# Sampled tokens' attention: all loads of cached values on SyncE's queue, between the key loads

## The reference

```python
def dilated_sample(q_a, k_a, v_a, k_buf, v_buf):      # branch A: 12 query heads, 4 K/V heads
    qg = q_a.reshape(DB, T, N_GROUPS_A, HEADS_PER_GROUP_A, HEAD_DIM)
    for g, (win, dil) in enumerate(DIL_PAIRS):         # (128, 1), (512, 4), (2048, 16)
        o, lse = dilated_gather_group(qg[:, :, g], k_a, v_a, k_buf, v_buf, win, dil)
    return merge_groups(outs, lses, q_a.dtype)

def dsa_sample(q_b, k_b, v_b, q_i, k_i, w_i, pool_k, pool_v, pool_ik, page_table):
    sc = ...                                           # indexer scores, the top 256 keys of each query
    ks = pool_k[phys, off]                             # branch B: paged cache, 8 query heads, 2 K/V heads
    vs = pool_v[phys, off]
    return sparse_attend(q_b, ks, vs, valid & (idx < P), k_b, v_b, sel_new)

o = (softmax(q k^T * HEAD_DIM ** -0.5 + mask)) @ v     # what each branch computes
x = x + gate * ((sigmoid(g_a) * ((o_a * silu(z_a)) @ w_pa) + sigmoid(g_b) * ((o_b * silu(z_b)) @ w_pb)) @ w_out)
```

## Time and profile before

| | us |
|---|---|
| median of 3 runs | 3146.28 |
| lowest and highest | 3145.56, 3151.08 |
| the execution that was profiled | 3147.91 |
| its span on the core | 3146.0 |
| PE busy in the span | 3054.7 (97%) |
| DVE, ACT, POOL busy | 1693.4, 749.9, 266.7 |
| stage of the sampled tokens | 2320 to 2461 |

### The profile page before, as it was taken

How to read it: one execution, slowest core, us unless ns; L and a number is a source line. 1 busy time by engine, 2 the same in 40 slices (tenths; PEclk the granted TensorE clock), 3 DMA queues, 4 the chain that set the end, 5 groups by cost and what they waited for, 6 DMA issues and landing times. The chain is left out here.

```text
span 3146.0 us, 50501 instructions
## 1 busy us (share of the span) xinstructions
PE 3054.7 (97%) x19803; PEld 2881.1 (92%) x19811; DVE 1693.4 (54%) x2463; ACT 749.9 (24%) x1173; POOL 266.7 (8%) x516
## 2 busy tenths in 40 slices
PE   5989999999999999999999999999999999999998
PEld 4869999999999999999999999988876897998986
DVE  4573786200786355555455554566654544654755
ACT  5240000011000111211111111165433323333333
POOL 3100000000000000000000000042224101010000
PEclk8999999999999999999999999999999999999999
DMA  9832222222222222333233232565269774683672
GB/s 350 282 114 70 75 74 61 82 61 61 82 75 61 94 63 75 105 93 102 75 95 109 81 102 75 181 198 147 85 188 312 215 269 158 194 269 127 207 237 98
DMA packets 452309, 425.08 MB, mean 135 GB/s; under 512 B 20628, under 2 KB 393620, under 8 KB 449108
## 3 DMA queue, kind: packets, MB, share of 16 engines
q1 hardware_dynamic: 428998, 343.06, 36.8%
q0 software_dynamic: 22048, 78.45, 6.7%
q10 hardware_dynamic: 1152, 2.13, 0.2%
HBM read 348.79 MB, written 76.88 MB: 135 GB/s over the span
## 5 line engine op out<-in xcount | busy, mean ns | idle before, releaser
L293 PE MATMUL banks<-h_hi,w_hi 128*128 128x352 f32 (+1 forms) x3552 | 1162.5, 327 | 0.0
L295 PE MATMUL banks<-h_hi,w_lo 128*128 128x352 f32 (+1 forms) x3552 | 1158.3, 326 | 0.0
L294 PE MATMUL banks<-h_lo,w_hi 128*128 128x352 f32 (+1 forms) x3552 | 1157.4, 326 | 0.0
L293 PEld LDWEIGHTS banks<-h_hi,w_hi 128*128 128x128 f32 x3552 | 666.8, 188 | 3.1 <-issue 3.0
L294 PEld LDWEIGHTS banks<-h_lo,w_hi 128*128 128x128 f32 x3552 | 669.2, 188 | 0.0
L295 PEld LDWEIGHTS banks<-h_hi,w_lo 128*128 128x128 f32 x3552 | 666.2, 188 | 0.0
L284 DVE TENSOR_TENSOR w_lo<-w_raw,w_hi 128x2048 fp32r<-128x2048 f32 x77 | 175.4, 2278 | 657.3 <-ACT w_hi L279 519.6
L372 ACT ACTIVATE col<-banks 128x384 f32<-128x384 f32 x150 | 71.2, 474 | 1023.6 <-PE banks L295 984.0
L1944 DVE TENSOR_TENSOR u_lo<-u_raw,u_hi 128x1536 fp32r<-128x1536 f32 (+1 forms) x96 | 196.4, 2046 | 200.4 <-ACT u_hi L1858 200.0
L2216 DVE MAX8 best<-work 128x8 f32<-128x1088 f32 x224 | 289.1, 1291 | 10.0
L2218 DVE MATCH_REPLACE8 work<-best,work 128x1088 f32<-128x1088 f32 x224 | 285.9, 1276 | 0.0
(11 more groups left out here) (313 smaller groups left out, 3432.0 us busy)
## 6 DMA issues: line engine op xcount, KB each, us to landing
w_raw<-in_w_in SPq DMA_DIRECT2D x76, 1024.0 KB, 5.5
u_raw<-in_w_out SPq DMA_DIRECT2D x96, 512.0 KB, 5.0
scratch_proj<-col POOLq DMA_DIRECT2D x76, 544.0 KB, 3.0
ada_w<-in_w_ada SPq DMA_DIRECT2D x16, 2048.0 KB, 13.9
u_raw<-in_w_pb SPq DMA_DIRECT2D x48, 512.0 KB, 4.9
gate_w<-in_w_ada SPq DMA_DIRECT2D x16, 1024.0 KB, 7.8
u_raw<-in_w_pa SPq DMA_DIRECT2D x48, 256.0 KB, 3.1
gates<-scratch_proj SPq DMA_DIRECT2D x64, 192.0 KB, 2.4
```

What stands on the lines that cost most here:

```text
L293: nc.tensor.matmul(dst, w_hi[:, par, k, 0:width], h_hi[:, k, a:b], start=(k == 0), stop=False)
L294: nc.tensor.matmul(dst, w_hi[:, par, k, 0:width], h_lo[:, k, a:b], start=False, stop=False)
L295: mm = nc.tensor.matmul(dst, w_lo[:, par, k, 0:width], h_hi[:, k, a:b], start=False, stop=(k == KT - 1))
```

## The change

Value sets 1 to 6 are issued by SP and no longer by POOL. SP's order becomes keys 2, values 1, keys 3, values 2, and so on to keys 7, values 6; o_raw, z_raw and values 7 follow as before. Values b still wait for `so_done` >= b-1, now in SP's queue; values 1 wait for `pv_done`, the end of the prompt's value products, for which POOL waited before it. All value sets count on one pair of semaphores, and PE waits on it for (half + 1) sets of the buffer, half being the sequence number divided by 2. POOL keeps `prepare`. The transfers, their sizes and destinations are the same, and PE's, ACT's and DVE's work too.

```diff
@@ load_values
             if not isinstance(b, int) or b >= 2:
                 sp.wait_ge(so_done, b - 1)
-            by_sp = isinstance(b, int) and b in (0, NB - 1)
-            load_rows(sp, b, par, (win_v, "cache_win_v"), (pool_v, "cache_v"), v_raw_landed if by_sp else v_next_landed)
+            load_rows(sp, b, par, (win_v, "cache_win_v"), (pool_v, "cache_v"), v_raw_landed)
@@ sp_sample
-            for b in range(2, NB):
+            load_keys(sp, 2, 0)
+            sp.wait_ge(pv_done, NJ)
+            load_values(sp, 1, 1)
+            for b in range(3, NB):
                 load_keys(sp, b, b % 2)
+                load_values(sp, b - 1, (b - 1) % 2)
             sp.wait_ge(att_stored[0], 16 * QT // 2)
@@ pool_sample
             prepare(1, 1, 0, False)
-            load_values(pool, 1, 1)
             with pool.Fori(1, NB // 2 - 1) as i:
                 for u in range(2):
                     prepare(2 * i + u, u, i, False)
-                    load_values(pool, 2 * i + u, u)
             prepare(NB - 2, 0, NB // 2 - 1, False)
-            load_values(pool, 2 * (NB // 2 - 1), 0)
             prepare(NB - 1, 1, NB // 2 - 1, False)
@@ pe_sample, body
-                if isinstance(b, int) and b in (0, NB - 1):
-                    pe.wait_ge(v_raw_landed[par], RAW)
-                else:
-                    pe.wait_ge(v_next_landed[par], (half + par) * RAW)
+                pe.wait_ge(v_raw_landed[par], (half + 1) * RAW)
```

More of the change, by code:

```diff
@@ L1269, in decode_step @@
         v_raw_landed = [sem(f"v_raw_landed{i}") for i in range(2)]
-        v_next_landed = [sem(f"v_next_landed{i}") for i in range(2)]
         prep_set = sem("prep_set")
```

## The result

| | us |
|---|---|
| changed kernel, median of 4 runs | 3177.23 (3173.99 to 3179.71) |
| kernel before, median of 4 runs | 3147.14 (3145.56 to 3151.08) |
| ratio | 1.0093, 95% interval 1.0080 to 1.0106 |
| changed kernel, the execution profiled, its span | 3173.99, 3172.1 |

The changed kernel is slower by 25 to 33 us (the interval of the ratio, in us). The forecast was 3173 us, +26.5, with a range of 3163 to 3186.

The account below looks back on a forecast made before the run. SP's issuing, 11.3 us a set, was taken to become the attention stage's bound. First matmul of the merge +25.5 us, from pace and tail, plus 1 for the clock: +26.5 on 3146.3, giving 3173 us, range 3163 to 3186.

Parts of the forecast that it names:

- The bound passes to SP's issuing: Sampled tokens' attention: SP needs 22.6 us per sequence against PE's 16.2, so its issuing replaces PE and DMA engines as bound.
- The new waits cost nothing: SP's queue: waits on so_done and pv_done are already met when SP reaches them, so they add no time.
- Which sets come late: Attention stage: keys 3 in time, values 2 at 2371.0 (wanted 2370.6), keys 4 at 2382.3 (wanted 2377.8), each set after waited for.
- The tail: After o_raw's issue at 2458.9: o_raw, z_raw and values 7, 7.34 MB at 362 GB/s, landing at 2480; term -6 to +10.
- pace: SP's issuing from keys 2 on: 12 sets at 11.3 us, 135.6 us, ending at 2458.9; term -2.4 to +13.
- From values 7 to the merge: From sequence 7's value products at 2480 to the merge's first matmul at 2487, +25.5 us against 2461.5 before.
- the 1 us for the clock: Allowance for slower PE work after waits, not hidden behind the last wait, before values 7: 1 us, between 0 and 4.
- Rival 1: Attention stage: DMA engines stay the bound, the queue is of no account, 3144 to 3152 us; chance 0.05.
- Rival 2: Attention stage: issuing sets in order of use saves 7 us, 3139, if SP issues a set under 8.1 us; chance 0.05.
- Rival 3: Attention stage: SP's sets stretch to 17.2 us each as in the kernel before, 71 us more, 3244 us; chance 0.07.
- The rule weighed: For these sets, issuing (11.3 us) outlasts moving (8.7 us at 302 GB/s), against the rule that sequencer time is usually small.

Follow-up runs that it names:

- What was added to the queue: Changed kernel, but SP loads each page number of value sets 1 to 6 into a register twice: 3204.81 us, ratio 1.0177 to the kernel before.
- fixed pages: Changed kernel with constant page numbers and no register loads from sequence 1 on, so other pages of the same size are read: 3155.33 us, ratio 1.0017.
- registers reused: Changed kernel, but page numbers loaded once per sequence, at its key set, serve its value set too: 3156.16 us, ratio 1.0027; again 3157.92 us, 1.0028.

## Why the prediction was right

- **The bound passes to SP's issuing: right.** Set pace 11.37 us against 11.3, 136.4 us for the 12 sets against 135.6. What was added to the queue (27 us) came through as 24 to 26 us, and of what was taken from it (o_raw 22.8 us sooner) 21 us were gained, so this is shown.
- **The new waits cost nothing: right.** SP shows no wait on `so_done` between keys 2 and o_raw.
- **Which sets come late: right for the keys, wrong for the values.** Keys 3 in time, values 2 late by 0.44 us where 0.4 was worked out, keys 4 by 5.05 where it was 4.5. But PE never waited for values 3 to 6, and I had said that it would. PE needs 9.8 us from the turning to the values' products at full clock; after each wait the 24 transposes took 4.5 to 5.4 us and not 2.8, which makes 11.6 to 12.5 us, over SP's 11.37. The slow clock took the place of the second wait. It changed nothing in the sum, since SP sets the pace.
- **The tail: mis-sized.** From o_raw's issue to the start of the values' products of sequence 7 I had 21.1 us, from 7.34 MB at 362 GB/s. It was 26.2 (2456.35 to 2482.58). In 2456 to 2483 the engines moved 8.55 MB at 317 GB/s:

```profile
DMA packets 7142, 8.55 MB, mean 317 GB/s; under 512 B 324, under 2 KB 6500, under 8 KB 7140
GB/s 138 59 194 71 337 398 400 403 416 360 364 369 373 375 369 373 376 371 373 371 378 374 353 230 241 176 224 285 331 349 355 361 349 355 339 321 297 294 292 275
```

  So two things were left out. 1.2 MB more moved, mostly the end of values 6 and the start of u_raw, which SP issued from 2476 on. And 362 GB/s held only from the fifth of these 40 slices to the 23rd, where o_raw and z_raw moved; the first four (2.7 us) stood at 59 to 194, and the five behind them, where by the order of the queue values 7 begin, at 176 to 285. This term is 5.1 us short. From the forecast's +26.5 one comes to the measured +30.5 of the stage with pace +0.8, tail +5.1, and -1.9 of the next item.
- **From values 7 to the merge: right, a little high.** 6.1 us, against 7 and the 1 us for the clock. That 1 us does not show: the first products of sequence 7 took 2.79 us, against 2.34 before, both partly or wholly at the lower level.
- **Rival 1, no difference:** what it needs is a set in 8.7 us. With fixed pages SP issued the first sets in 6.8 and 7.4 us, the DMA share was 1.04 again, and the loss 2 to 9 us. As a mechanism it is nearly right once SP keeps up, and that was not the case here. **Rival 2, use order:** its condition, SP's own pace under 8.1 us, was met in that same kernel and nothing was gained; the lower rate there leaves open what the order is worth by itself. **Rival 3** did not occur in the changed kernel, whose sets never stretched while the engines were not full. With fixed pages, where the engines were full, they did stretch, to 9.8 us each (2333.99 to 2431.99, ten sets).
- **The rule weighed** (the Trainium skill, DMA: Bandwidth & Descriptors, "Issuing engines are not separate DMA queues"): that all issuing engines feed the same 16 DMA engines agrees with a share of 1.04 from SP's queue alone, and with the 2 to 9 us that the queue still made once issuing was cheap. That the issue time is usually small was not so for these sets: 11.3 us to issue what the engines move in 8.7, eight pages of 128 KB, each behind a register load.

**Open.** Why the value sets on SP's queue cost another 2 to 9 us with the issuing out of the way. The rate goes with it: 277 GB/s with nothing on POOL, 284 with a fifth of the bytes, 292 to 295 with 45% or more. Packet size alone does not give this row (1.83 and 1.87 KB stand for 284 and 295, and 2.11 for 292), and neither does the number of queues in use, which is two in all but the first. How the two queues share the engines was not tried by itself.

## What to carry to other kernels

Before transfers are gathered on one engine, add up what it takes that engine to issue them, register loads included, and compare the sum per step with the step of the engine that waits; below it such moves cost 1 to 9 us here and not 30, above it what was added showed nearly in full. A queue's own timeline in a stretch where nothing blocks it gives this pace, and busy times do not show it at all. And a wait removed by another order of the same bytes can turn up again at the transfer that is now last, as it did twice here, with z_raw.

## What the runs showed that was not expected

- A second register load right behind another costs SP 0.57 us (4.5 us for eight), while the whole step of a page is 1.1.
- At a DMA share of 1.05 to 1.06 the engines moved 277, 284, 292 or 295 GB/s in the same stretch, and 362 where o_raw and z_raw moved. With the registers reused they moved 279 at a share of 0.95. At full share the rate is not one number.
- After waits of 3.7 to 5.1 us PE's next 24 transposes took 4.5 to 5.4 us and not 2.8. Around two of them the granted clock was 0.57 (2378 to 2384) and 0.52 (2400 to 2406), the level of 1.2 GHz for most of it.
